# Moving the split weights, the token parts and the hidden parts to other byte positions in SBUF

## The reference

```python
h = layer_norm(ALPHA * h + diff_attention(h, w_in, w_o))      # 272 tokens, 1024 -> 3072, 1024 -> 1024
h = layer_norm(ALPHA * h + swiglu(h, w_gate, w_up, w_down))   # 1024 -> 2816 -> 1024
h = layer_norm(ALPHA * h + rwkv7_time_mix(h, w_rkv, ...))     # 3 x (1024 -> 1024), scan, 1024 -> 1024
h = layer_norm(ALPHA * h + moe_swiglu(h, router, w_gate, w_up, w_down))  # 8 experts, 1024 -> 3584 -> 1024
x = h[:, 16:]                                                 # 256 tokens from here on
x = x + mla_and_retention(x); x = x + conv_ffn(x, 0)          # conv_ffn: 1024 -> 2 x 2816 -> 1024
x = x + gla(x);               x = x + conv_ffn(x, 1)
```

## The kernel before, in words

| buffer | byte address | phase |
|---|---|---|
| con (constants) | 57152 | 64 |
| sh0, sh1, sl0, sl1 | 71136 and every 12288 on | 224 |
| xh0 / xh1 / xl0 / xl1 | 120288 / 129440 / 138592 / 147744 | 224 / 160 / 96 / 32 |
| arena, ffn_h, conv_h, moe_h, conv_l, moe_l | 156896 (h), 179424, 159968 | 224 |
| ffn_l | 180832 | 96 |
| sh2, sl2, down3 | 163040 on | 224 |

## Time and profile before

### The profile page before, as it was taken

One profiled execution on the slowest core, in us unless ns is written; L12 is line 12 of the kernel. 1 busy time (PEld: TensorE's weight loads), 2 busy tenths in 40 slices (PEclk: granted clock), 3 DMA queues, 4 the chain that ended last, 5 costly groups with the idle time before them and its releaser, 6 DMA issues.

```text
span 2699.8 us, 58833 instructions
## 1 busy us (share of the span) xinstructions
PE 2554.3 (95%) x25616; PEld 2366.9 (88%) x25616; DVE 2032.6 (75%) x3184; ACT 1565.4 (58%) x2516; POOL 51.1 (2%) x58
## 2 busy tenths in 40 slices
PE   7999999978878999999999999999988899999999
PEld 7779998856766899999999999999887699988999
DVE  5455547785545599999999999999866788575884
ACT  4335434473223477777777777777755566464662
POOL 0001100000000000000000000000003000000000
PEclk9889999977798999999999999999999999999999
DMA  6113442200001399999999999999833245441453
GB/s 251 57 71 118 184 176 96 99 1 4 20 5 65 108 338 356 338 354 345 342 357 341 354 336 361 337 360 342 332 115 113 72 172 185 168 179 57 179 176 121
DMA packets 83274, 538.71 MB, mean 200 GB/s; under 512 B 9488, under 2 KB 9616, under 8 KB 38976
## 3 DMA queue, kind: packets, MB, share of 16 engines
q1 hardware_dynamic: 82368, 530.68, 53.6%
q0 software_dynamic: 640, 4.19, 0.4%
HBM read 533.79 MB, written 1.05 MB: 198 GB/s over the span
## 4 chain that ended last, share of the span: by engine, by line
PE 85%; DVE 8%; ACT 4%; issue 2%; DMA 0%; DVEq 0%; ACTq 0%; SPq 0%; PEldq 0%
PE ps L568 23%; PE ps L569 23%; PE ps L570 23%; PE ps L574 1%; DVE sl L530 1%; PE ps L1425 1%; PE ps L1936 1%; PE ps L1410 1%; PE ps L1419 1%; PE ps L583 1%; PE ps L1384 1%; PE ps L806 1%; DVE xl L564 1%; ACT sh L523 1%; PE ps L2080 1%
## 5 line engine op out<-in xcount | busy, mean ns | idle before, releaser
L2163 DVE TENSOR_TENSOR sl<-ring,sh 128x1024 fp32r<-128x1024 f32 x613 | 735.3, 1220 | 29.1 <-ACT sh L2121 18.1
L2121 ACT ACTIVATE sh<-ring 128x1024 fp32r<-128x1024 f32 x613 | 630.5, 1053 | 1.9 <-DVE xl L2006 1.9
L568 PE MATMUL ps<-sh,xh 128*128 128x256 f32 (+2 forms) x2012 | 591.3, 294 | 10.3 <-DVE sl L530 9.5
L570 PE MATMUL ps<-sh,xl 128*128 128x256 f32 (+2 forms) x2012 | 571.8, 284 | 0.0
L569 PE MATMUL ps<-sl,xh 128*128 128x256 f32 (+2 forms) x2012 | 571.7, 284 | 0.0
L568 PE MATMUL ps<-xh,sh 128*128 128x256 f32 (+2 forms) x1856 | 535.4, 288 | 26.3 <-DVE sl L530 14.6
L569 PE MATMUL ps<-xl,sh 128*128 128x256 f32 (+2 forms) x1856 | 530.5, 286 | 0.0
L570 PE MATMUL ps<-xh,sl 128*128 128x256 f32 (+2 forms) x1856 | 527.3, 284 | 0.0
L530 DVE TENSOR_TENSOR sl<-ring,sh 128x1024 fp32r<-128x1024 f32 (+1 forms) x341 | 399.6, 1198 | 68.8 <-ACT sh L523 68.4
L523 ACT ACTIVATE sh<-ring 128x1024 fp32r<-128x1024 f32 (+1 forms) x341 | 338.8, 1021 | 112.4 <-PE ps L570 105.9
L568 PEld LDWEIGHTS ps<-sh,xh 128*128 128x128 f32 x2012 | 379.5, 189 | 21.3 <-DVE sl L530 4.7
(11 more groups left out here) (568 smaller groups left out, 3998.9 us busy)
## 6 DMA issues: line engine op xcount, KB each, us to landing
ring<-ws_d SPq DMA_DIRECT2D x229, 1024.0 KB, 7.1
ring<-ws_d SPq DMA_DIRECT2D x80, 1536.0 KB, 6.4
ring<-ws_d SPq DMA_DIRECT2D x225, 512.0 KB, 6.7
ring<-ws_d SPq DMA_DIRECT2D x24, 1408.0 KB, 6.0
ring<-ws_d SPq DMA_DIRECT2D x4, 1256.0 KB, 5.4
ring<-ws_d SPq DMA_DIRECT2D x2, 1088.0 KB, 4.9
scan_t<-scn_d POOLq DMA_DIRECT2D x1, 1824.0 KB, 7.4
ring<-ws_d SPq DMA_DIRECT2D x1, 1248.0 KB, 5.3
```

The source lines that it names most:

```text
L568: e.matmul(out, ah, bh, start=start, stop=False)
L570: return e.matmul(out, al, bh, start=False, stop=stop)
L2121: e.activation(out, raw(u)[:, a:z], ACT.Copy).then_inc(*af.on("high", u, i))
L2163: e.tensor_tensor(l, raw(u)[:, a:z], f32(h), SUB).then_inc(s_fd if i < 2 else s_fp, 1)
```

## The change

`XW` grows from 2288 to 2304 columns (9216 bytes, a multiple of 256). `pos` and `flag` (64 bytes together) go from ahead of `xt` to the end. A gap of 16 columns (64 bytes) stands between the split weights and the token parts. `XO` names the place of the token parts in `scan_t`, and the views that lie over them follow. The experts take their tokens 112 columns (448 bytes) into the token parts, and the token slices for them too. No instruction is added, removed or reordered, apart from that.

```diff
-        par_t, con_t, pos_t = sb("par", [128, np_]), sb("con", [128, nc_]), sb("pos", [128, 8], i32)
-        flag_t = sb("flag", [128, 8], i32)[:, 0:1]
+        par_t, con_t = sb("par", [128, np_]), sb("con", [128, nc_])
         xt = sb("xt", [128, 8 * T0])
         AB = 8 * T0
-        XW = AB + 112
-        NL = 2 * SLOTS * BW + 4 * XW
-        NA = (208 * 1024 - 512 - 4 * (RING * BW + np_ + nc_ + 16 + AB + NL)) // 4 // 16 * 16
+        XW = AB + 128
+        XO = 2 * SLOTS * BW + 16
+        NL = XO + 4 * XW
+        NA = (208 * 1024 - 192 - 4 * (RING * BW + np_ + nc_ + 16 + AB + NL)) // 4 // 16 * 16
...
             sl = [sb(f"sl{i}", [128, BW], f32r, c) for i in range(SLOTS)]
+            sb("between", [128, 16], fp32, c)
             xh = [sb(f"xh{i}", [128, XW], f32r, c) for i in range(2)]
...
         arena = sb("arena", [128, NA])
+        pos_t = sb("pos", [128, 8], i32)
+        flag_t = sb("flag", [128, 8], i32)[:, 0:1]
...
-        XF = [cut(scan_t, 2 * SLOTS * BW + XW, 8, T0), at(tail_o + AB + 4 * T0, 8, T0)]
+        XF = [cut(scan_t, XO + XW, 8, T0), at(tail_o + AB + 4 * T0, 8, T0)]
...
+        MO = 112
...
         def by_token(v, j):
-            return v[j][:, 1024:2048]
+            return v[j][:, MO + 1024:MO + 2048]
...
         def gathered(e):
-            return [v[e % 2][:, 0:1024].rearrange("p (k t) -> p k t", k=8) for v in (xh, xl)]
+            return [v[e % 2][:, MO:MO + 1024].rearrange("p (k t) -> p k t", k=8) for v in (xh, xl)]
```

More of the change, by code:

```diff
@@ L1748, in build @@
         rs = at(tail_o + 1024, T0)
-        YG, SQ = (cut(scan_t, 2 * SLOTS * BW + i * XW, 8, T0) for i in (1, 3))
+        YG, SQ = (cut(scan_t, XO + i * XW, 8, T0) for i in (1, 3))
         x_ro = Parts("rwkv out", 0, 8, T0, 1)
@@ L1888, in gathered @@
         def gathered(e):
-            return [v[e % 2][:, 0:1024].rearrange("p (k t) -> p k t", k=8) for v in (xh, xl)]
+            return [v[e % 2][:, MO:MO + 1024].rearrange("p (k t) -> p k t", k=8) for v in (xh, xl)]
         def routed(e):
-            return [v[e % 2][:, 0:1024].rearrange("p (a b) -> p a b", a=2) for v in (xh, xl)]
+            return [v[e % 2][:, MO:MO + 1024].rearrange("p (a b) -> p a b", a=2) for v in (xh, xl)]
         def router_pe(w, e):
@@ L2210, in many_pe @@
         def many_pe(w, e):
-            xm_h, xm_l = (v[0][:, 0:XA].rearrange("p (k t) -> p k t", k=8) for v in (xh, xl))
+            xm_h, xm_l = (v[0][:, MO:MO + XA].rearrange("p (k t) -> p k t", k=8) for v in (xh, xl))
             def up(u):
@@ L2243, in many_act @@
         def many_act(w, e):
-            xm_h = xh[0][:, 0:XA].rearrange("p (k t) -> p k t", k=8)
+            xm_h = xh[0][:, MO:MO + XA].rearrange("p (k t) -> p k t", k=8)
             for k in range(0, 8, 2):
@@ L3069, in build @@
         o += 8 * T
-        g_x0, g_x2 = 2 * SLOTS * BW, 2 * SLOTS * BW + 2 * XW
+        g_x0, g_x2 = XO, XO + 2 * XW
         KEs = [at(o, 4, T), cut(scan_t, g_x2, 4, T)]
```

## The result

The kernel after takes 2712.22 us (median of 15 runs, 2701.17 to 2724.54), the kernel before 2701.14 us beside it (15 runs, 2690.72 to 2711.63). The ratio is 1.0036, 95% interval 1.002 to 1.0051: 0.36% slower where 0.7% faster was forecast.

A forecast was written before the change was run, and what follows sets the result against it. The prediction took PE's pitch in the large matmuls, set by the phases of its two operands, as the bound. Dense products 16.7 us plus experts 2.0 gave 18.7 us less, 2678.3 us; 8-in-10 range 2667 to 2702.

The forecast's parts named there:

- rival 1: Whole kernel: addresses don't matter and nothing moves, 2697 us; chance 0.09.
- That is the pair of two of the three matmuls of an odd expert's step: Dense 256-column products: weights at 160 and moving parts at 224 were taken to give 114 ns a matmul.
- Up products: Two convolutional layers, 2112 matmuls: from 117.65 to 114 ns each, 7.7 us gained.
- Down products: Two convolutional layers, 1056 matmuls: from 119.9 to 114 ns each, 6.2 us gained.
- 256-column tiles of the mixing layers: Two mixing layers, 984 matmuls: 3.6 us gained by pitch, 2.8 counted because of waits for splits and norms.
- Experts: Expert layer: 2.0 us gained, between 5.1 gained if the stationary place counts and 5.1 lost at worst.
- If it is the difference of the two phases that counts: Experts: two units in three slow at 120 ns, one fast; at worst all eight take 127.74 us, 5.1 us lost.
- the 1.28 us: Experts: even ones at 127.74 us against odd ones at 126.46, a gap held smaller because odd ones wait for splits.
- 272-column products: Dense products, 2928 matmuls: the round of four phases starts elsewhere, 0 us; ends 5 gained and 15 lost.
- On the path, as nothing else in these windows is near its limit: Dense 256-column products: their 16.7 us all shorten the run, with VectorE at 102/116 after the change.
- Rival 2: Dense products settle at 117.65 ns; only 2.4 us there and 2.0 in the experts gained, 2692.5 us; chance 0.14.
- Rival 3: High and low parts sharing a phase slow 3096 matmuls by 2.25 ns; experts lose too, 2709 us; chance 0.16.

The follow-up runs named there:

- e1: Kernel before with experts' tokens at eight places, high and low parts 128 bytes apart, and both convolutional layers' tokens moved; 2700.56 us, one run, beside 2701.84.
- e4: Kernel before with only the even experts' tokens moved to phases 160 and 32, those of the odd experts; 2693.06 us, ratio 0.9965.
- e11: Kernel after with the weights' low parts 128 bytes on from the high parts (160 and 32), dense tokens at 96; 2709.84 us, one run.
- e12: e11 with the convolutional hidden parts at 96 too and the experts' tokens at six pairs of places; 2703.33 us, one run, beside 2695.71 of kernel before.
- e5: Kernel after with experts' tokens at 96 (high) and 224 (low), and sh2 moved to 160 like the other split weights; 2706.18 us, ratio 1.0015.
- e2: Kernel before with high and low token parts in one phase and experts' tokens at eight places; 2715.32 us, one run, beside 2701.84 of kernel before.
- e9: e5 with the experts' hidden parts moved to 160 too; 2696.36 us, one run, beside 2701.00 of kernel before.

## Why the prediction was wrong

**What stood.** The reading of the bound was right: the pitch of the large matmuls sets the time, and it follows the phases of the two operands. e1, e4 and e11 show that with every instruction kept the same; e4's 0.9965 is such a gain. The Trainium skill, page "SBUF — State Buffer", section "SBUF: two separate sides", has PE never wait on anyone on the engine side, by which such a change would do nothing (rival 1). The runs don't agree: 1021 and 1056 matmuls in 120 us differ in addresses alone.

**The step that failed** is "That is the pair of two of the three matmuls of an odd expert's step; the third there had its next stationary at 32, so the pattern isn't quite the same. I take 114 ns". It priced a matmul by the phases of its own pair, and the third matmul was waved off. The runs show the fast rate with the whole step in place: a moving operand at one place and a stationary one that goes to and fro, 64 bytes to either side (odd experts, e4, e11, e12). The change took all high and low parts to one phase, and with that removed the going to and fro everywhere. The kernel after has the good pair alone, (160, 224), in the experts' units that use `sh2`: 117.8 ns in the mean, against 115.4 in an odd expert before; its units on `sh0` and `sh1`, with (160, 160), have 118.9. By terms of the sum:

- Up products, 7.7 us forecast: 0.00 in both layers and both profiles. The 118 ns before (tokens less weights 0, 128, 0 in the first layer and 192, 64, 192 in the second) and after (64, 64, 64) are the same slow rate by different places.
- Down products, 6.2 us forecast: 2.3 us in the first profile and 4.7 in the second. (224, 224) was the 120 ns of the worst case, and its going is the one real gain of the change. Whether a layer then gets 118 or 113 ns is left to its start.
- The 256-column tiles of the mixing layers, 2.8 us forecast: next to nothing. The mean pitch stayed at 117.8 ns in the even layer and went from 117.8 to 117.1 and 116.4 ns in the odd one's some 600 matmuls, 0.4 to 0.8 us. The odd layer's stage went up 2.9 to 4.6 us with 17 and 21 us of low clock, and was 153.65 us in e5, with 7. The dense placement is the same in all three.
- Experts, 2.0 us gained forecast, 5.1 lost as the worst end: 4.3 to 4.7 lost over the six periods measured, 1.4 for each of three odd experts and 0.1 for each even one. At that rate all eight lose 6, just beyond the worst end; the value was on the wrong side. The text had named the case ("If it is the difference of the two phases that counts"), but gave it less weight than a stationary place that counts by itself, which e2's expert 2 doesn't support (tokens at 160, 117.2 ns). Its reason for the 1.28 us, that the odd experts already wait for splits, isn't borne out either: the list of waits has none of PE in the periods of experts 1 and 2 of the kernel before. The 6.7 ns was the settled rate against a slow spell; the means differ by 3.2 ns, 2.2 us over 672 matmuls. The experts' 512-column products, taken at nothing, went from 231.8 to 232.6 ns.
- 272-column products, 0 forecast with 5 gained to 15 lost: some 2 us lost. The token products' mean pitch goes from 125.1 to 126.1 ns over some 2,300 matmuls, and it is 126.1 in each kernel whose token parts share one phase and whose weights share one (e2, e5 and e9 too); their round of twelve takes 1.52 us in place of the 1.50 of the earlier trace rows.
- All else, 0 forecast: the instructions that write `xl` and `xh` have medians of 1217 and 1018 ns (1218 and 1018 in the earlier trace rows), and the two forms of the earlier trace rows 255 and 252 ns in place of 253 and 245, in a stage that differed by 15 us between two executions of one kernel.

The pitches account for some 4 to 6 us in all (experts 6, 272 columns 2, down products 2.3 to 4.7 the other way), against the 7 to 8 at equal clock; the rest isn't placed.

Had the first terms been right, the sum would still have been too large. "On the path, as nothing else in these windows is near its limit" failed in e11: at 113 ns the up product gave 3.1 us for two layers in place of 7.7, because a mean busy share of VectorE of 102 in 120 us says nothing of the last tiles, where the split of the next weights stands behind the last hidden values.

**The rivals.** Rival 2 had the condition right ("The 114 needs the alternation between 160 and 32 that the odd experts have") and the dense products' result; it then added a gain in the experts, where the same condition had just been removed. Rival 3 had the sign and nearly the size, 2709 against a median of 2712, and the loss in the experts, but not the mechanism: the down products became faster, not slower, and its deciding point (up products above 118 ns) wasn't met. Two conditions that the prediction held apart, the alternation of rival 2 and the shared phase of rival 3, are two sides of one arrangement: parts in one phase can't alternate.

**What stays open.** Why the place itself counts when all differences are equal (e9 settles only in the first half of a unit, e4 in both), what chooses between 118 and 113 ns at the start of a down product of one and the same program, and why the granted clock was lower in the runs of the kernel after. No run here separates them. A version with alternating stationary weights in the dense layers and one fixed phase for the experts' weights wasn't tried.

## What to carry to other kernels

When one instruction form has two rates in a trace, compare whole steps, the order of operands included, before the rate is carried over to another place, and take the mean over a stage rather than the best spell in a timeline. The cheap edit is the one that copies the fast pattern to its slow twin (e4: even experts like odd ones, 5.2 us, ratio 0.9965); a layout that looks tidier and keeps only part of the pattern can lose it everywhere. And before a faster engine is put down as a gain, look at the one wait at the end of its stage: what PE saves there may only be waited for.

## What the runs showed of the hardware that was not expected

- Dense products of 256 columns in float32r with a weight load for each matmul ran at one of three rates, at full clock and with nothing but addresses changed: 113 to 114, some 118, or 120 ns (1056, 1021 and 1002 in 120 us). Those of 272 columns ran at 125.1 to 125.3 ns with high and low token parts 128 bytes apart, at 126.1 with both in one phase, and at 125.5 with the weights' parts 128 bytes apart instead (e11, e12).
- With the experts' token parts 128 bytes apart, the sweep looks the same after 128 bytes: weights less high tokens of 64 and of 192 have 115.5 and 115.7 ns, all others 118.0 to 118.9. With both parts in one phase it doesn't (117.2 and 116.4, 119.6 and 118.0).
- The rate has a memory. It settles over three to six matmuls after a break in the experts (e4), and one program's down product took 62.26 us in one execution and 59.92 in the next.
- A wait of 1.4 us ahead of the down product left the clock at its upper level (0 of 528 matmuls slow), one of 3.7 us was followed by 15 and 16 matmuls at 213 ns in the two layers of e11.
- The scan's stage took 332.7 and 317.2 us in two executions of the kernel after, with 154 and 126 us at the lower clock. A difference of that size between two profiles says nothing of a change; a table by stage, with the time at the lower clock beside each, does.
